# Hybrid decoder step on one core: matrix products over 1032 columns cut as 512 + 512 + 8 instead of three pieces of 344

## The reference, cut to what matters

```
xn = RMSNorm(x);  [qA|kA|vA|cq|ckv|kpe|gA|gB] = xn @ W_in
h  = x + W_o( sigmoid(gA) * (DilatedAttn(qA,kA,vA) @ P_A) + sigmoid(gB) * (MLA(cq,ckv,kpe) @ P_B) )
h += MemCrossAttn(RMSNorm(h), mem)       # 4 heads over 256 memory tokens
h += relu(RMSNorm(h) @ W_up)^2 @ W_down  # squared-ReLU MLP
y = RMSNorm_final(h)
```

## Time and profile before

| | us |
|---|---|
| three timed runs | 2568.49, 2571.34, 2575.53 |
| median of them | 2571.34 |
| span of the profiled execution, first to last instruction | 2576.4 |
| PE busy in it | 2304.4 |
| DVE busy in it | 1016.8 |

### The profile page before, as it was taken

The page is one execution under the profiler, slowest core; times in us unless marked ns, Lnnn a source line. Parts: engine busy times, 40 slices in busy tenths (PEclk is TensorE's granted clock), DMA queues, the critical chain, the costliest instruction groups (busy, mean ns, idle before and its releaser), DMA issues. The chain is left out here.

```text
span 2576.4 us, 39191 instructions
## 1 busy us (share of the span) xinstructions
PE 2304.4 (89%) x15432; PEld 2029.4 (79%) x15432; DVE 1016.8 (39%) x1453; ACT 550.9 (21%) x970; POOL 114.0 (4%) x222
## 2 busy tenths in 40 slices
PE   6999988938999689887699989877999999999997
PEld 6999966825566566665688879756899999999997
DVE  4221235563566445454222232455531431422423
ACT  3000014411333233332011121232310110110111
POOL 0000000000200122221000000000000000000000
PEclk8999958659999899999799999896899999999998
DMA  5113131030991478886411111120211111111111
GB/s 181 49 41 123 39 111 56 30 108 19 309 333 44 142 232 238 245 240 162 173 45 45 45 43 36 66 90 1 58 50 50 42 50 50 41 50 42 50 50 74
DMA packets 231621, 247.95 MB, mean 96 GB/s; under 512 B 29748, under 2 KB 216092, under 8 KB 230222
## 3 DMA queue, kind: packets, MB, share of 16 engines
q1 hardware_dynamic: 216530, 214.45, 27.5%
q0 software_dynamic: 8976, 31.57, 3.8%
q10 hardware_dynamic: 5996, 0.25, 0.2%
HBM read 220.34 MB, written 69.87 MB: 113 GB/s over the span
## 5 line engine op out<-in xcount | busy, mean ns | idle before, releaser
L1156 PE MATMUL ps<-mats,mla_rows 128*128 128x128 f32 x1024 | 130.2, 282 | 49.7 <-DMA mla_rows<-in_cache_mla 49.3
L2323 PE MATMUL ps<-xn_hi,mlp_w_hi 128*128 128x344 f32 x768 | 164.1, 322 | 7.7 <-DVE mlp_w_lo L2137 5.3
L1156 PEld LDWEIGHTS ps<-mats,mla_rows 128*128 128x128 f32 x1024 | 115.0, 145 | 64.8 <-issue 38.3
L2323 PE MATMUL ps<-mlp_xn_lo,mlp_w_hi 128*128 128x344 f32 x768 | 163.7, 321 | 0.0
L2323 PE MATMUL ps<-u_lo,mlp_w_hi 128*128 128x344 f32 x768 | 163.0, 320 | 0.0
L2323 PE MATMUL ps<-xn_hi,mlp_w_lo 128*128 128x344 f32 x768 | 162.9, 320 | 0.0
L2323 PE MATMUL ps<-u_hi,mlp_w_hi 128*128 128x344 f32 x768 | 162.9, 320 | 0.0
L2323 PE MATMUL ps<-u_hi,mlp_w_lo 128*128 128x344 f32 x768 | 162.1, 319 | 0.0
L2323 PEld LDWEIGHTS ps<-xn_hi,mlp_w_hi 128*128 128x128 f32 x768 | 129.8, 190 | 9.2 <-DVE mlp_w_lo L2137 6.4
L2323 PE MATMUL ps<-xn_hi,win_hi 128*128 128x344 f32 x576 | 123.1, 322 | 7.8 <-DVE win_lo L2588 7.8
L2323 PEld LDWEIGHTS ps<-u_lo,mlp_w_hi 128*128 128x128 f32 x768 | 130.0, 189 | 0.0
(11 more groups left out here) (372 smaller groups left out, 4032.0 us busy)
## 6 DMA issues: line engine op xcount, KB each, us to landing
mla_rows<-in_cache_mla SPq DMA_DIRECT2D x384, 144.0 KB, 3.1
out_s_dsa_w<-in_cache_dsa_w SPq DMA_DIRECT2D x8, 4094.0 KB, 82.2
mla_rows<-in_cache_mla POOLq DMA_DIRECT2D x128, 144.0 KB, 2.6
oaT<-in_w_up SPq DMA_DIRECT2D x32, 512.0 KB, 4.2
oaT<-in_w_down SPq DMA_DIRECT2D x32, 512.0 KB, 3.9
obT<-in_w_in SPq DMA_DIRECT2D x23, 512.0 KB, 3.7
gate_w<-in_w_in SPq DMA_DIRECT2D x16, 512.0 KB, 4.1
out_s_dsa_w<-in_cache_dsa_w SPq DMA_DIRECT2D x8, 1022.0 KB, 17.6
```

Source lines behind the costliest of these rows:

```text
L1156: last = nc.tensor.transpose(ps[:, 2 * (g % 2) + c, j * P:(j + 1) * P], rows[:, v, 4 * g + j, c * P:(c + 1) * P], ident)
L2323: last = nc.tensor.matmul(out[:, t, 0:TC], w, x[:, k, t * TC:(t + 1) * TC], start=first, stop=stop)
```

## The change

A table `COLS` of start and width replaces the equal pieces in `product3` and `branch_product`: 512 columns to the first bank of a set, 512 to the second, and the remaining 8 to the third. Since the first two banks are now full, the 1032 results lie in one run, and `banks` and `psv` view this run instead of the first 344 columns of each bank. The view keeps its shape of 3 times 344, so the DVE instructions keep their form. The numbers of matmuls, of weight loads and of columns, the terms, their order and all semaphores stay. Other products over 1032 columns (L725, L735, the norm sums) keep their three equal pieces.

```diff
+COLS = ((0, 512), (512, 512), (2 * 512, T - 2 * 512))
...
     def banks(s):
-        return ps[:, 3 * s:3 * s + 3, 0:TC]
+        return ps[:, 3 * s:3 * s + 3, :].rearrange("p a n -> p (a n)")[:, 0:T].rearrange("p (a t) -> p a t", a=NT)
...
                         for k in range(kc):
-                            for t in range(NT):
-                                last = nc.tensor.matmul(ps[:, 3 + t, 0:TC], wp[:, j, k, :],
-                                                        src[:, k, t * TC:(t + 1) * TC], start=(k == 0),
+                            for t, (lo, n) in enumerate(COLS):
+                                last = nc.tensor.matmul(ps[:, 3 + t, 0:n], wp[:, j, k, :],
+                                                        src[:, k, lo:lo + n], start=(k == 0),
                                                         stop=(k == kc - 1))
...
-                for t in range(NT):
-                    last = nc.tensor.matmul(out[:, t, 0:TC], w, x[:, k, t * TC:(t + 1) * TC], start=first, stop=stop)
+                for t, (lo, n) in enumerate(COLS):
+                    last = nc.tensor.matmul(out[:, t, 0:n], w, x[:, k, lo:lo + n], start=first, stop=stop)
...
             def psv(s):
-                return ps[:, 3 * s:3 * s + 3, 0:TC]
+                return ps[:, 3 * s:3 * s + 3, :].rearrange("p a n -> p (a n)")[:, 0:T].rearrange("p (a t) -> p a t", a=NT)
```

## The result

The changed kernel takes 2863.34 us, median of 4 runs (2854.97 to 2869.42), against 2569.91 us for the kernel before (4 runs). The ratio is 1.1139, with an interval of 1.1114 to 1.1164: 11.4% slower. The prediction was 2873 us, in a range of 2774 to 2955.

A forecast was written before the change was run, and what follows sets the result against it. PE's row of instructions was taken to bound the changed stages. Triplets +295.1, branch products +9.9 and waits -2.9 gave +302 us on 2571.3: 2873 us, 11.7% slower, range 2774 to 2955.

The forecast's parts named there:

- The 14.4 ns: MLP's 344-column float32r matmuls: time beyond 143.3 ns of 2.4 GHz streaming, taken as proportional; 233.6 ns per 512; chance 0.43.
- a fixed cost: Rival in product3: the extra 14.4 ns falls once per matmul, triplet 567.4 ns, kernel 2841 us; chance 0.25.
- quick streaming: Rival in product3: 512 columns take only 215.7 ns, with 112 for the tail, kernel 2774 us; chance 0.06.
- The tail costs a bare load: product3's 8-column matmul holds PE for an unhidden weight load, 112 ns; triplet 579.2 ns, +295.1 us over 2784.
- Branch products: 48 groups of float32 products, each going from 1734 to 1940 ns: +9.9 us.
- Waits: Gate stage: growth of the first gate and branch products goes into PE's existing waits, -2.9 us.
- Bank reads at nothing: DVE's reads of the result banks keep the same rate, 1225 ns against 1228, counted as 0.
- my own key: Reading of MLP start distances: 234, 234, 112 expected; 228 fixed cost, 216 quick streaming, 158 longer load, 6 to 25 load ahead.
- the longer load path: Rival in product3: the load behind the tail takes 157.7 ns instead of 112, kernel 2904 to 3005 us; chance 0.16.
- load plus streaming: Rival in product3: loads and streaming add up, so a triplet costs the same as before, 2571 us; chance 0.02.
- the free tail: Rival in product3: the load after the tail is taken in ahead, tail 5.6 ns, kernel 2470 us; chance 0.04.
- The clock: Rival in the changed stages: clock falls to 1.2 GHz for a tenth of the triplets, kernel 3009 us; chance 0.04.

The follow-up runs named there:

- e3: Changed kernel with product3's 8-column matmul run only in the first triplet of each chunk, left out of 2662 others: 2570.41 us, ratio 0.9996.
- e7: Changed kernel with product3's 8-column tail streaming its columns 43 times over, 344 columns: 2953.97 us, ratio 1.1493.
- e8: Kernel before, each 344-column piece in product3 streaming the same 8 columns 43 times: 2474.92 us, ratio 0.9632.
- e11: Kernel before, the MLP's normalised input holding the same 8 columns of values over and over at different addresses: 2569.07 us, one run.
- e4: Changed kernel, the 8-column matmul using only 64 of 128 weight columns in 2540 of 2784 product3 triplets: 2866.28 us, ratio 1.1163.
- e5: Changed kernel, the first 512-column matmul using only 64 of 128 weight columns in 2540 of 2784 product3 triplets: 2733.76 us, ratio 1.0644.
- e6: Changed kernel with product3's 8-column tail streaming its columns 29 times over, 232 columns: 2856.99 us, ratio 1.1112.
- e2: Kernel before with only the branch products cut into 512 + 512 + 8, product3 keeping pieces of 344: 2579.84 us, ratio 1.0041.
- e10: Kernel before, every weight load in product3 taking one weight column 128 times: 2570.05 us, ratio 0.9995.

## Why the prediction was right

*PE alone sets these stages.* Right: DVE, ACT and the clock are unchanged, and the time is in PE's rows.

*The 14.4 ns are slower streaming, in proportion to the columns, and no wait for weights.* Right in kind, and in size partly by luck. The 467.7 ns that 576.7 leaves beside the load of 109 is 233.9 for each 512, where I had 233.6; a fixed cost would have given 227.7 and quick streaming 215.7. But where no load is exposed a 512 stands at 232.0 (e3) or 231.7 ns (e7), below the proportion and above the fixed cost. Behind an exposed load the first long matmul takes 235.3, the second 232.4, and why the first is slower was not tried. e8 brings 157.7 down to 146.0 by repeating the columns, with the loads left as they are. My guess at the cause, a supply that keeps up with 1.2 columns per ns and not with 2.4, is what e8 to e11 leave standing.

*The tail costs a bare load.* The mechanism is right: e3 gives 110 ns per tail, e4 and e5 show that it is the next matmul's load, e6 that streaming below it is free. Its size was 112 ns, taken from 64-column float32 products; the loads behind the tails stand 108 or 109 ns apart. Why those products took 3 ns more is not shown. The triplet came out 2.5 ns under the forecast, x 2784 = 7 of the 10 us by which the time did; the interval of the ratio is 6 us either way.

*Branch products.* +9.9 us predicted, 10.5 measured alone (e2, 7 to 14 by its interval).

*Waits.* 2.9 us were to be absorbed. The wait of 9.93 us took up 1.7 of the 2.5. The wait for the gate's first weights went from 2.82 to 1.79 us, where 0.4 were forecast; the wait for a transfer ahead of the first branch product also shrank, from 4.4 to 3.0 us, with nothing of the change in front of it in this stage, so not all of such a difference is the change. Too small to see in the time.

*Bank reads at nothing.* Right, 1229 ns against 1228.

*The sum.* 2784 x 103.5 = 288.1 us, with the branches' 10 and the waits' -3 is 295; measured are 293.4. Two slips in the working move nothing: (5.28 - 0.354) / 23 is 214 and not 213, and the chances outside the range add up to 0.18 and not 0.17.

*What the profile would show.* The input projection's and W_o's windows came out at 335 and 114 us, where 336 and 112 were forecast, and the MLP's at 888 instead of 896, of which the triplet's 2.5 ns are 4; the wait fell to 8.26 and not to about 7. And here a step failed. I wrote that the starts of the matmuls would stand 234, 234 and 112 ns apart, and that 6 to 25 ns would mean a load taken in ahead. The recorded starts stand some 27 ns apart behind the tail and 0.32 us behind the first long matmul (2200.63 to 2200.95), close to what my own key calls a load taken in ahead. The loads' starts carry the pattern, and the load behind the tail does start as the tail goes, as forecast.

*The rivals.* The fixed cost falls by the 233.9 ns and by the 231.7 of e7, faster streaming by the same numbers, the longer load path by the 108 or 109 ns between the loads, load plus streaming by e6, the free tail by e3. The rule of the Trainium skill that a load overlaps only a matmul of other row groups ("TensorE: Matmul & The Clock Gate", "Part 3: Packing small matmuls — row/col tiling") is contradicted again by e6: 232 columns pass during the next load at no cost. The clock did not fall: it stayed at 0.98 to 1.00 in the four stages.

Is there a cut that beats both? None was tried. Three pieces of 344 each stream longer than a load and so hide all loads. Any cut into three must stream the same 1032 columns, and e3 shows how little is in it: even two matmuls for 1024 columns take 464 ns to the 473.2 of today's triplet, and the remaining 8 columns would have to cost less than 9 ns.

## What to carry to other kernels

Where every matmul loads its own weights, a matmul costs the longer of its streaming and the next one's load, so cut columns into pieces that all stream longer than a load. By an estimate from the rows here that takes about 240 columns of float32r, (109 - 2.3) / 0.452, or 128 of float32, (109 - 2.3) / 0.833; of such widths only 344 and 512 were run. Equal pieces then beat full banks with a remainder as short as the 8 columns here. Before you change widths, look at what stands behind each short matmul, and read the loads' starts and not the matmuls' to see where PE waits for weights.

## What the runs showed of the hardware

- A float32r matmul over different columns takes 157.7 ns for 344 and 233.9 for 512 in the changed kernel (231.7 in e7) at a granted clock of 1.00, some 8% more than 2.4 GHz and the 2.3 ns of the float32 rows give. With 8 columns repeated it takes 146.0 for 344 (e8). At 1.2 GHz nothing is lost (286.7 ns). Neither the weight load's addresses (e10) nor the streamed values (e11) change it.
- A tail of 8 and one of 232 columns cost the same (110 ns by e3, 522 and 524 instructions in 100 us), as both end under the next load of 128 weight columns; with 64 weight columns in that next load it is 51 ns less (e5), with 64 in the tail's own nothing less (e4).
